# Block-product pairs: weight units split by four instructions instead of seven, in another order, and the activations' block sums behind the last plain pair

## What is computed

```python
def swiglu(h, w_in, w_out):            # h: 512 x 1024
    gu = h @ w_in                      # w_in: 1024 x 5632
    gate, up = gu[..., :D_FF], gu[..., D_FF:]      # D_FF = 2816 = 22 chunks of 128
    return (jax.nn.silu(gate) * up) @ w_out        # w_out: 2816 x 1024
```

## Time and profile before

| | us |
|---|---|
| median of 3 runs | 1812.81 (1811.77 to 1815.83) |
| the profiled execution | 1810.08 |
| its span, first to last instruction | 1808.1 |
| busy: PE / PEld / DVE / ACT / POOL | 1762.2 / 1576.2 / 1354.4 / 838.8 / 31.2 |
| mean granted TensorE clock | 0.993 |
| DMA | 183.24 MB, 101 GB/s on average |

### The profile page before, as it was taken

The page is one execution under the profiler, slowest core; times in us unless marked ns, Lnnn a source line. Parts: engine busy times, 40 slices in busy tenths (PEclk is TensorE's granted clock), DMA queues, the critical chain, the costliest instruction groups (busy, mean ns, idle before and its releaser), DMA issues.

```text
span 1808.1 us, 31383 instructions
## 1 busy us (share of the span) xinstructions
PE 1762.2 (97%) x12746; PEld 1576.2 (87%) x12753; DVE 1354.4 (75%) x2110; ACT 838.8 (46%) x1581; POOL 31.2 (2%) x63
## 2 busy tenths in 40 slices
PE   9999999999999999999999999999999999999999
PEld 7789899897698799899887998998887987998998
DVE  6788488579767888497578884875887778875874
ACT  5445345355844455255344452553424443552552
POOL 0000000023000000000000000000000000000000
PEclk9999999999999999999999999999998999999999
DMA  6332323322032323233323232333354223332231
GB/s 201 103 117 94 117 94 106 117 66 90 3 104 70 117 94 117 88 99 108 104 70 116 94 117 84 103 104 107 111 165 130 94 79 108 105 106 93 96 116 47
DMA packets 74440, 183.24 MB, mean 101 GB/s; under 512 B 23712, under 2 KB 30512, under 8 KB 74304
## 3 DMA queue, kind: packets, MB, share of 16 engines
q1 hardware_dynamic: 72128, 179.02, 30.7%
q0 software_dynamic: 1600, 1.52, 0.3%
q10 hardware_dynamic: 576, 0.79, 0.1%
HBM read 174.35 MB, written 6.29 MB: 100 GB/s over the span
## 4 chain that ended last, share of the span: by engine, by line
PE 57%; DVE 23%; ACT 12%; issue 6%; DMA 0%; DVEq 0%; ACTq 0%; SPq 0%
PE bank L514 12%; PE bank L516 12%; PE bank L515 12%; PE bank L855 7%; DVE w_lo L1542 5%; ACT w_hi L1156 5%; PE bank L607 4%; DVE w_raw L1550 4%; DVE r_pre L1553 2%; PE bank L612 2%; DVE w_lo L1526 2%; DVE up_tmp L1809 2%; ACT a_hi L1308 1%; DVE gate_tmp L1789 1%; ACT gate_tmp L1298 1%
## 5 line engine op out<-in xcount | busy, mean ns | idle before, releaser
L514 PE MATMUL bank<-a_hi,w_hi 128*128 128x512 f32 (+1 forms) x912 | 337.1, 370 | 17.2 <-DVE a_lo L1620 16.1
L515 PE MATMUL bank<-a_lo,w_hi 128*128 128x512 f32 (+1 forms) x912 | 335.5, 368 | 0.0
L516 PE MATMUL bank<-a_hi,w_lo 128*128 128x512 f32 (+1 forms) x912 | 335.3, 368 | 0.0
L855 PE MATMUL bank<-x_hi,w_hi 128*128 128x256 f32 x1024 | 292.5, 286 | 15.8 <-ACT sq_tmp L1292 15.8
L855 PE MATMUL bank<-x_lo,w_hi 128*128 128x256 f32 x1024 | 289.6, 283 | 0.0
L855 PE MATMUL bank<-x_hi,w_lo 128*128 128x256 f32 x1024 | 289.4, 283 | 0.0
L1542 DVE TENSOR_TENSOR w_lo<-w_raw,w_hi 128x512 fp32r<-128x512 f32 x384 | 251.8, 687 | 37.8 <-ACT w_hi L1156 36.6
L1526 DVE TENSOR_TENSOR w_lo<-w_raw,w_hi 128x1024 fp32r<-128x1024 f32 x142 | 173.8, 1224 | 103.2 <-ACT w_hi L1108 102.8
L1108 ACT ACTIVATE w_hi<-w_raw 128x1024 fp32r<-128x1024 f32 x142 | 147.7, 1052 | 212.8 <-PE bank L516 200.2
L1156 ACT ACTIVATE w_hi<-w_raw 128x512 fp32r<-128x512 f32 x384 | 218.2, 621 | 30.4 <-PE bank L516 30.4
L855 PE MATMUL bank<-raw_forms_hi,w_lo 128*128 128x256 f32 x768 | 215.8, 281 | 0.0
(11 more groups left out here) (245 smaller groups left out, 2913.8 us busy)
## 6 DMA issues: line engine op xcount, KB each, us to landing
w_raw<-stream SPq DMA_DIRECT2D x312, 512.0 KB, 3.3
h_resid<-xT SPq DMA_DIRECT2D x8, 256.0 KB, 5.9
qT<-stream SPq DMA_DIRECT2D x8, 256.0 KB, 6.1
u_scratch<-V SPq DMA_DIRECT2D x8, 256.0 KB, 3.1
a_lo<-u_scratch SPq DMA_DIRECT2D x8, 256.0 KB, 2.9
qT<-z_scratch SPq DMA_DIRECT2D x8, 256.0 KB, 4.3
outT<-h_resid SPq DMA_DIRECT2D x10, 128.0 KB, 1.7
z_scratch<-kT SPq DMA_DIRECT2D x2, 256.0 KB, 4.3
```

The source lines that it names most:

```text
L514: nc.tensor.matmul(out, lw[0], lx[0], start=first, stop=False)
L515: nc.tensor.matmul(out, lw[0], lx[1], start=False, stop=False)
L516: return nc.tensor.matmul(out, lw[1], lx[0], start=False, stop=last)
L855: last = nc.tensor.matmul(out, left, right, start=(product in (UP1, UP2, UP5) and k + j == 0), stop=(k == KD // 2 - 1 and j == 2), skip_gr ...
```

## The change

It has four parts.

1. A pair's seven units are split by four instructions on each of ScalarE and VectorE. `units_hi` and `units_lo` (with `units_from`, `units_to`) take UP1 and UP2 together, UP5 and UP7 together, UP6 alone, UP3 and UP4 together. The places in `w_hi`/`w_lo` are rearranged so that each such set is contiguous there, and TensorE and SyncE wait for split numbers instead of unit numbers.
2. The order in a round of `pairs` is another on ScalarE and VectorE. UP5 and UP7 come right after the first sum, ahead of UP6; on ScalarE the copy of UP6's sum stands ahead of the last split, and in the first round of a group ahead of the split of UP6's unit too; on VectorE `first_up` stands ahead of the unit of UP6. In the last round the second down slot is split behind `first_up`.
3. The three raw forms of ScalarE are made behind the weight split of pairs 3 and 4 instead of after pairs 2 and 3; each waits for the half of the normalised blocks that it reads.
4. The four block sums of the activations are all made behind the last plain pair, instead of two after pair 4 and two after pair 5.

The diff, cut to its core:

```diff
-PLACE_OF = {UP1: 0, UP2: 1, UP6: 2, UP5: 3, UP7: 4, UP4: 5, UP3: 6}
+PLACE_OF = {UP1: 0, UP2: 1, UP5: 2, UP7: 3, UP6: 4, UP3: 5, UP4: 6}
+SPLIT_OF = {UP1: 0, UP2: 0, UP5: 1, UP7: 1, UP6: 2, UP3: 3, UP4: 3}
+SPLITS = 4
...
+        def units_from(pair, split):
+
+            blocks = raw[:, 2 * (pair % 2):2 * (pair % 2) + 2, :].rearrange("p a (b n) -> p (a b) n", b=2)
+            return (blocks[:, 0:4:3, :], blocks[:, 0:2, :], third_sum[:, None, :], blocks[:, 2:4, :])[split]
...
# SyncE, load
-                    sp.wait_ge(s_ulo, 7 * pair + (7 if second else 5))
+                    sp.wait_ge(s_ulo, SPLITS * pair + (4 if second else 2))
# ScalarE, pair_steps
                 if not first:
                     next_slot(n, s)
+                if chunk == 3:
+                    form_hi(q // KF, UP1, 0, HALVES[0])
+                    form_hi(q // KF, UP2, 1, HALVES[0])
+                if chunk == 4:
+                    form_hi(q // KF, UP4, 1, HALVES[1], -1.0)
# ScalarE
+            def units_hi(pair, split):
+
+                if split:
+                    act.wait_ge(s_usum, 3 * pair + split)
+                nc.scalar.activation(units_to(w_hi, pair, split), units_from(pair, split), ACT.Copy).then_inc(s_uhi, 1)
# ScalarE, pairs
-                        unit_hi(ahead, UP1, 0)
-                        unit_hi(ahead, UP2, 3)
+                        units_hi(ahead, 0)
...
-                        act.wait_ge(s_usum, 3 * ahead + 2)
-                        unit_hi(ahead, UP6, None)
+                        units_hi(ahead, 1)
+                        if i == 0:
+                            seen_of(pair, UP6, 1)
+                        units_hi(ahead, 2)
+                    else:
+                        down_hi(n0 + 1, 1, pair - 1, UP7)
                     silu_first(pair)
-                    if more_pairs:
-                        unit_hi(ahead, UP5, 0)
-                        unit_hi(ahead, UP7, 1)
-                    else:
-                        down_hi(n0 + 1, 1, pair - 1, UP5)
                     if i:
                         silu_second(pair - 1)
-                    seen_of(pair, UP6, 1)
+                        seen_of(pair, UP6, 1)
                     if more_pairs:
-                        act.wait_ge(s_usum, 3 * ahead + 3)
-                        unit_hi(ahead, UP4, 3)
                         if i:
                             act.wait_ge(s_up, multiplied(pair - 1, UP3))
-                        unit_hi(ahead, UP3, 2)
+                        units_hi(ahead, 3)
# VectorE, pairs
-                        unit_lo(ahead, UP1, 0)
-                        unit_lo(ahead, UP2, 3)
+                        units_lo(ahead, 0)
                         unit_sums(ahead)
+                        units_lo(ahead, 1)
                     else:
                         down_lo(n0, 0)
                     first_gate(pair)
+                    if i:
+                        first_up(pair - 1)
                     if more_pairs:
-                        unit_lo(ahead, UP6, None)
-                        unit_lo(ahead, UP5, 0)
-                        unit_lo(ahead, UP7, 1)
-                        unit_lo(ahead, UP4, 3)
+                        units_lo(ahead, 2)
                     else:
                         down_lo(n0 + 1, 1)
                     if i:
-                        first_up(pair - 1)
                         product(pair - 1)
                     if more_pairs:
-                        unit_lo(ahead, UP3, 2)
+                        units_lo(ahead, 3)
# VectorE, ffn
                     if p == 4:
                         form_lo(UP4, 1, B, negative=True)
-                        dve.wait_ge(s_flo, FORMS * index + 3)
-                        summed_x(4 * index, (1, B), (0, B), (1, B), ALU.add)
-                        summed_x(4 * index + 1, (0, B), (0, A), (0, B), ALU.subtract)
-                    if p == 5:
-                        summed_x(4 * index + 2, (0, A), (1, B), (0, A), ALU.subtract)
-                        summed_x(4 * index + 3, (1, A), (1, A), (0, A), ALU.subtract)
+                dve.wait_ge(s_flo, FORMS * index + 3)
+                summed_x(4 * index, (1, B), (0, B), (1, B), ALU.add)
+                summed_x(4 * index + 1, (0, B), (0, A), (0, B), ALU.subtract)
+                summed_x(4 * index + 2, (0, A), (1, B), (0, A), ALU.subtract)
+                summed_x(4 * index + 3, (1, A), (1, A), (0, A), ALU.subtract)
```

More of the change, by code:

```diff
@@ L350, in blk, with unit, units_to @@
             return slot(ring, s)[:, k * width:(k + 1) * width]
-        def unit(w, pair, product):
+        def unit(w, pair, product, count=1):
             at = PLACE_OF[product] * UNIT
-            return w[:, pair % 2, at:at + UNIT]
+            return w[:, pair % 2, at:at + count * UNIT]
+        def units_from(pair, split):
+            blocks = raw[:, 2 * (pair % 2):2 * (pair % 2) + 2, :].rearrange("p a (b n) -> p (a b) n", b=2)
+            return (blocks[:, 0:4:3, :], blocks[:, 0:2, :], third_sum[:, None, :], blocks[:, 2:4, :])[split]
+        def units_to(w, pair, split):
+            first, count = ((UP1, 2), (UP5, 2), (UP6, 1), (UP3, 2))[split]
+            return unit(w, pair, first, count).rearrange("p (b n) -> p b n", b=count)
         def raw_block(pair, i):
@@ L1181, in first_pair_units @@
                 act.wait_ge(s_mm, n0 + 5)
[L1182 to L1183 removed]
+                units_hi(pair, 0)
                 act.wait_ge(s_mm, n0 + 6)
[L1185 to L1191 removed]
+                units_hi(pair, 1)
+                units_hi(pair, 2)
+                units_hi(pair, 3)
             def down(n0, last_of=None, pair=None, index=None):
```

48 lines of the change are left out of this document (11 added, 37 removed).

## The result

| | before | after |
|---|---|---|
| median (us) | 1812.29 of 4 runs (1810.06 to 1815.83) | 1768.46 of 4 runs (1766.83 to 1772.06) |
| the profiled execution (us) | 1810.08 | 1766.83 |
| its span (us) | 1808.1 | 1765.0 |
| mean granted TensorE clock | 0.993 | 0.997 |

The ratio of after to before is 0.9759, with a 95% interval of 0.9737 to 0.9782. The change takes 43.8 us off the medians and 43.1 us off the spans; 45 were forecast, and a median of 1767.5.

A forecast was written before the change was run, and what follows sets the result against it. TensorE, busy 97%, bounds the kernel, so only its waits or slow clock pay: 23.6 (plain pairs) - 0.4 + 21.6 (pairs) = 44.8 us off, 1765.3 for the profiled execution, median 1767.5; range 1762 to 1783.

The forecast's parts named there:

- Plain pairs, 5.9 less 0.1 per FFN: End of plain pairs: TensorE's `a_lo` wait and slow matmuls go, 5.9 us per FFN; 0.1 charged at down slot 4.
- First wait of a group: Pair 0 of each group: TensorE's wait before UP7 goes because UP6's sum is copied earlier, 1.44 us per group.
- Three late gaps: Pairs 4, 5 and 6 of each group: TensorE's gaps before UP7 go, 1.46 us per group.
- The rings' margin: Pair rounds: the rings of waits through ScalarE stay about 0.5 us under TensorE's 10.02 us per pair.
- Ring B: Pair rounds: closed ring of waits through TensorE, UP6's copy, UP7, its sum's copy and the first split, 9.55 us.
- Pair 1, charged at 0.2: Pair 1 of each group: starts from a late round, its UP7 0.1 to 0.2 us late; 0.2 charged.
- The last pair: Last pair of a group: second down split behind first up on VectorE; second up still in time for UP3, costing nothing.
- The rule on instruction cost: VectorE splits: by the skill's page each merge saves 157 ns, 0.47 per round, making merging the steady gain's cause.
- Rings longer than summed: Rival, pair rounds: a ring of 10.4 us or more leaves the three late gaps, 1779 us; chance 0.13.
- The plain wait only shrinks: Rival, plain pairs: VectorE still late at the last bank, costing 1.5 to 4 us per place, say 1780; chance 0.13.
- Slower and nothing: Rivals: a far costlier ring B, 1842 us, chance 0.03; both waits replaced by equal ones, 1812, chance 0.04.
- The forecast's two signs: No TensorE `a_lo` wait; VectorE rounds 10.0 us apart, idle before first up. Also `sq_tmp` waits 32 to 8 or none.

The follow-up runs named there:

- the order alone: Kernel before with the new pair-round order but seven 512-column splits kept, plain pairs as before: 1793.28 us, ratio 0.9896.
- the merging alone: Kernel before with four splits instead of seven in the old order, plain pairs as before: 1800.29 us, ratio 0.9936.
- the padded kernel with 256 columns: Changed kernel with the last round's second down split ahead of the first up, plus a 256-column ScalarE copy ahead of UP6's copy in rounds 1 to 6: 1767.21 us.
- the mended kernel: Changed kernel with VectorE's second down split ahead of the first up in each group's last round: 1763.25 us, ratio 0.9732.
- 0.73 us more: Changed kernel with the last round's second down split ahead of the first up, plus a 768-column ScalarE instruction ahead of UP6's copy in rounds 1 to 6: 1784.18 us.
- either part by itself: Kernel before with only the four sums behind the last plain pair: 1795.46 us; with only the raw forms behind the weight splits: 1792.22 us.

## Why the prediction was right, and where not

**The sum** of 44.8 us stands against 43.1 of span, and the predicted 1767.5 against 1768.5. The small miss is made of one step that failed and terms that were a little off on both sides. (1812.8 less 44.8 is 1768.0; the 1767.5 on record is half a microsecond lower than its own sum.)

- *Plain pairs, 5.9 less 0.1 per FFN: right.* Measured 5.83, 5.76, 5.62 and 5.79 in the four FFNs. The times of the chain came out within 0.4 us: last scaling at 73.23 (73.45 forecast, and 1.15 us of idle time before it: VectorE was ready at 72.1, 72.4 forecast), `a_lo` at 75.35 (75.68), sums from 77.44 to 82.44 (77.78 to 82.75), first down split of ScalarE at 86.33 (86.65). The first matmul of down slot 4 (89.36) takes 0.34 to the next instead of 0.23, 0.11 late, as charged.
- *First wait of a group: right.* Gone in all 8 groups, and back when its one copy is put back.
- *Three late gaps: right, by the cause given.* VectorE and ScalarE set the pace at 10.49 and now follow TensorE at 10.00. The two single-part kernels show what the diff cannot: the order alone gives 2.40 us per group, and the merging alone gives 1.64, but with the first wait kept and no room left. One gap was missed in the earlier trace rows's stretch: a small one ahead of the three, at pair 3, worth 0.14 us per group (two matmuls 0.19 from the next instead of 0.12). So 3.04 per group were to be had, not 2.9.
- *The rings' margin: right.* Ring B summed to 9.55 and measured 9.63; had it been 0.5 longer, the padded kernel with 256 columns (0.31 more) would already have waited in every pair, and it did so only at pair 1.
- *Pair 1, charged at 0.2: too much.* The first matmul of its UP7 (121.49) takes 0.18 to the next instead of 0.12, so 0.06.
- *The last pair, "the second up ends at about 11.2 us of the round, and UP3 is due at 11.4: nothing": this step failed.* The arithmetic on UP3 held, but I followed the delay to the wrong customer. The first up of the last round cannot start before TensorE has made UP3 of the pair before, so what is queued behind it on VectorE (down split, then product) starts late however early VectorE is free: it idles 3.79 us there. From the product the delay goes over `a_hi` on ScalarE to the copy of UP7's sum behind it, and TensorE wants that for UP4, which is ahead of UP3 in its list. The gap is 0.68 instead of 0.12, and the matmul after it 0.19 instead of 0.12: 0.63 us in each group, 5.0 in all, and the mended kernel gave just that back (80.64 to 80.01 us per group, 5.2 by the medians).

With these in place a group's account closes: 3.04 - 0.06 - 0.63 = 2.35, as measured. That the total came so close is partly luck. The miss of 5.0 us was partly hidden by three small ones on the other side: the overcharged pair 1 (8 x 0.14 = 1.1), the missed gap (8 x 0.14 = 1.1) and the 1.2 outside the changed places.

**The rule on instruction cost.** The earlier trace rows show two narrow splits back to back in 1.28 us, and the wide one takes 1.23: merging two saves 0.05 us. The Trainium skill (VectorE: DVE Perf Modes, TRN2 errata) gives an fp32 `tensor_tensor` of N columns (N + 151) / 0.96 ns; the 151 cycles are by estimate 157 ns for each instruction. Its duration of a single one agrees (0.69 for 512 columns, 1.22 for 1024); what I drew from it, 157 ns for each merge, does not come, since back-to-back instructions here overlap. The cause that it suggested, merging rather than order, falls for the round: merging alone gave 10.14, order alone 10.00. Merging alone did remove the three late gaps all the same, because 10.14 is short enough for a group of eight.

**The rivals.** Rings longer than summed: did not come; 0.73 us more brings it, 0.31 more does not. The plain wait only shrinks: did not come, but either part by itself would have given it (1795 and 1792 without the gain of the pairs). Slower and nothing: did not come. The forecast's two signs (no `a_lo` wait, rounds 10.0 apart with VectorE idle before the first up) both showed; "32 to 8 short ones or none" came as none on `sq_tmp`, and 8 on `sum_sq`, where I had not looked.

## What to carry to other kernels

When two engines feed a third, add up each closed ring of waits for one round, and compare it with the round of the engine that should lead; the longest ring, not the busiest engine, tells what a reordering is worth. When an instruction is moved ahead of another, ask first what it waits for: a step that has to wait for the lead engine holds everything behind it, so work that is ready belongs in front of it, in the last round too, where other work takes the places of the loop's. Follow each delay through every queue it passes to every consumer on the lead engine, in the order of that engine's list, and not only to the consumer of the moved step's own result.
